# A diffusion block and a state-space block on one core: the turn of the attention probabilities moved to a third step of its unit

## The reference, cut to what matters

```python
for l in range(DEPTH):                    # DEPTH = 2
    with_ctx = l < DEPTH - 1              # 256 context tokens take part as queries in layer 0 only
    p  = jnp.split(n @ w_in[l], split_points, axis=-1)
    pc = jnp.split(nc @ w_in[l], split_points, axis=-1)
    oa, oa_c = diff_attention(...)          # "diff": two softmaxes per head, subtracted
    ob, ob_c = window_attention(...)        # "win": 2 key heads, a sink logit
    on, on_c = neighborhood_attention(...)  # "na": bias and mask
    od, od_c = qknorm_attention(...)        # "qk": normed q and k, 2 key heads
    y = (jnp.concatenate([oa, ob, on, od], axis=-1) * jax.nn.silu(p[12])) @ w_out[l]
    h = h + gate[:, None] * rms_norm(y, post_norm_g[l])
```

## Time and profile before

| | |
|---|---|
| median of 3 runs | 3108.85 us (3107.84 to 3115.51) |
| the profiled execution, its own time | 3112.07 us |
| its span in the profile | 3110.3 us |
| mean granted TensorE clock | 0.958 |
| PE busy | 2926.6 us, 94% of the span |
| DVE, ACT, POOL busy | 1937.8, 1164.8, 354.0 us |

### The profile page before, as it was taken

How to read it: one execution, slowest core, us unless ns; L and a number is a source line. 1 busy time by engine, 2 the same in 40 slices (tenths; PEclk the granted TensorE clock), 3 DMA queues, 4 the chain that set the end, 5 groups by cost and what they waited for, 6 DMA issues and landing times. The chain is left out here.

```text
span 3110.3 us, 40412 instructions
## 1 busy us (share of the span) xinstructions
PE 2926.6 (94%) x15557; PEld 2367.4 (76%) x15557; DVE 1937.8 (62%) x3393; ACT 1164.8 (37%) x1870; POOL 354.0 (11%) x317
## 2 busy tenths in 40 slices
PE   7989899999989997999999999989999999999998
PEld 2447677787767775868787777755789999999886
DVE  3238778676777767462445557875866666666444
ACT  3233332323323334242433443333344444444443
POOL 5760000000000000000000003532400000000000
PEclk9999999999999998999999998985899999999999
DMA  9846246353344564333333454420244555555554
GB/s 337 277 147 233 96 139 203 104 172 107 123 141 163 191 235 159 132 100 106 117 114 109 138 169 139 137 93 19 90 149 152 181 183 190 184 180 189 194 191 154
DMA packets 154592, 484.79 MB, mean 156 GB/s; under 512 B 17168, under 2 KB 18192, under 8 KB 153232
## 3 DMA queue, kind: packets, MB, share of 16 engines
q1 hardware_dynamic: 139968, 439.42, 42.2%
q10 hardware_dynamic: 14432, 42.79, 4.0%
HBM read 469.03 MB, written 13.11 MB: 155 GB/s over the span
## 5 line engine op out<-in xcount | busy, mean ns | idle before, releaser
L1484 DVE TENSOR_TENSOR split_weights<-common,split_weights 128x1024 fp32r<-128x1024 f32 x644 | 797.5, 1247 | 599.2 <-ACT split_weights L2211 551.5
L2211 ACT ACTIVATE split_weights<-common 128x1024 fp32r<-128x1024 f32 x644 | 671.4, 1052 | 812.6 <-PE bank L1160 752.1
L1158 PE MATMUL bank<-split_weights,features 128*128 128x512 f32 x1920 | 807.4, 421 | 48.9 <-DVE split_weights L1484 19.5
L1160 PE MATMUL bank<-split_weights,features 128*128 128x512 f32 x1920 | 760.7, 396 | 0.0
L1159 PE MATMUL bank<-split_weights,features 128*128 128x512 f32 x1920 | 760.0, 396 | 0.0
L1158 PEld LDWEIGHTS bank<-split_weights,features 128*128 128x128 f32 x1920 | 367.9, 192 | 163.7 <-issue 48.6
L1160 PEld LDWEIGHTS bank<-split_weights,features 128*128 128x128 f32 x1920 | 367.0, 191 | 80.7
L1159 PEld LDWEIGHTS bank<-split_weights,features 128*128 128x128 f32 x1920 | 368.1, 192 | 78.3 <-issue 11.3
L1607 DVE CUSTOM_DVE_ANT_0 common<-first_block_work,common 128x512 f32<-128x512 f32 x448 | 336.2, 751 | 92.3 <-DMA first_block_work<-w_mod_cols 75.1
L1158 PE MATMUL bank<-ffn_input_split,split_weights 128*128 128x256 f32 (+1 forms) x1376 | 389.8, 283 | 0.8 <-issue 0.8
L1160 PE MATMUL bank<-ffn_input_split,split_weights 128*128 128x256 f32 (+1 forms) x1376 | 389.0, 283 | 0.0
(11 more groups left out here) (295 smaller groups left out, 3396.3 us busy)
## 6 DMA issues: line engine op xcount, KB each, us to landing
common<-w_in SPq DMA_DIRECT2D x260, 512.0 KB, 3.4
common<-w_up SPq DMA_DIRECT2D x172, 512.0 KB, 4.3
first_block_work<-w_mod_cols SPq DMA_DIRECT2D x256, 256.0 KB, 3.8
common<-w_out SPq DMA_DIRECT2D x104, 512.0 KB, 3.3
common<-w_down SPq DMA_DIRECT2D x84, 512.0 KB, 3.4
old_stream<-w_mod SPq DMA_DIRECT2D x64, 512.0 KB, 4.7
trig<-common ACTq DMA_DIRECT2D x32, 272.0 KB, 4.4
second_block_work<-trig ACTq DMA_DIRECT2D x32, 272.0 KB, 2.7
```

The costliest lines, as they stand in the source:

```text
L1158: e.matmul(out_ap, xs[0], ws[0], start=first, stop=False)
L1160: return e.matmul(out_ap, xs[0], ws[1], start=False, stop=last)
L1484: e.tensor_tensor(lo, raw, hi.bitcast(F32), ALU.subtract).then_inc(*low_done.tick(("lo", m)))
L2211: e.activation(split_slots[:, 0, i, 0:words], raw_slots[:, m % RAW, 0:words], ACT.Copy).then_inc(*high_done.tick(("high", m)))
```

## The change

A unit of attention now comes in three steps: scores of unit i, then the values of unit i-2 (with `heads_out`), then the transposes of unit i-1. Pace, projections and all other work stay as they are. An attention has 54 steps in layer 0 and 30 in layer 1.

```diff
@@ -553,8 +553,6 @@
                     self.do("scores", n, l, g, kind, kvh, t, h, self.pb if biased else None)
             self.scale_heads()
             yield
-            if 0 <= i - 1 < len(units):
-                self.do("turn_probs", first + i - 1, units[i - 1][0], self.copies(), kind)
             if 0 <= i - 2 < len(units):
                 t, h = units[i - 2]
                 self.do("values", first + i - 2, l, g, kvh, t, h)
@@ -568,6 +566,9 @@
                     self.do("heads_out", first + i - 2, l, g, kind, t, r)
                     if kind == "diff":
                         self.unscaled.append(("heads_scaled", first + i - 2, l, g, t, r))
+            yield
+            if 0 <= i - 1 < len(units):
+                self.do("turn_probs", first + i - 1, units[i - 1][0], self.copies(), kind)
             yield
         self.scale_heads()
```

## The result

The change takes 3122.58 us in the median (12 runs, 3116.18 to 3128.71), the kernel before on the same chip 3110.03 us (12 runs, 3103.49 to 3115.95): ratio 1.0039, 95% interval 1.003 to 1.0049. It is slower by 12.5 us. The profiled execution of the change took 3128.71 us (span 3126.6, mean granted clock 0.954), 6 us above its median; that of before 3112.07 us, 2 us above. So between the two profiles lie 16.3 us of span, and I lean on a second profile of the change (span 3121.2) wherever a few us matter. Lines behind the edit are one higher in the change than before (1273 is now 1274). A "tail" is what is left of an attention when the products it hides between are through.

What follows compares the result with a forecast made beforehand. PE, busy 94% of the span, was taken to bound the kernel. Costs of 34.7 us, mostly tails, less a gain of 25 us gave +9.7 us: 3118.6 us in the median, range 3103 to 3136.

Steps and rivals of the forecast that it cites:

- Place 2's tail: End of layer 0's place 2 attention: 15.3 us of PE idle, first wait about 9 us, on ACT's copy.
- Rival A: Faster: tails flow, PE idles under 3 us in layer 0's place 2 tail; 3096 us, chance 0.11.
- What that tail saves later: After layer 0's place 2 tail: later PE waits on q's heads, 1.07 and 4.49 us, saved; 5.6 us.
- Place 3's tail: End of layer 0's place 3: about 17 us long, about 10 us idle; cost 9.0 us with the clock.
- Place 1: Layer 0's place 1: 3.8 us of its 4.9 us wait gained, tail costing 2.5 us.
- rival B: Waits stay because they come from DVE's backlog; gain 12 us for 25, time 3131 us; chance 0.15.
- Place 0: Layer 0's place 0: 4.7 us of waits gained, 1.9 of the 8.36 us scores' wait; tail costs 4.5 us.
- Layer 1: Layer 1's attention: waits of 4.8, 2.3 and 3.2 us gained in places 0 to 2; tails 5.3 and 2.2 us.
- The background "at nothing": Background's end moves from clock 1278 to about 1320, some 16 advances lost in layer 0; costed at nothing.
- rival C: Background dot products come later, where DVE feeds projections; 12 of 19 us show, 3131 us; chance 0.09.
- Rival D: Clock falls in every tail: 4 x 2.5 us more, 3129 us; chance 0.13.

Runs made afterwards that it cites:

- e3: The change with the steps left of layer 0's place 2 attention taken ahead of the first q tile's finish: 3103.37 us, 0.9984 of before.
- e11: The change with three more background advances, at clocks 701, 717 and 733 of layer 0, shifting every later row switch: 3106.6 us, 0.9993 of before.
- e4: Three steps only in layer 1's places 0 and 1, two steps everywhere else: 3100.19 us, 0.9973 of before.
- e8: e4 with the background held for the 24 clocks ahead of layer 0's places 0 and 1: 3083.32 us, 0.9922 of before.
- e2: The change with the background advanced at the clocks of the kernel before: 3123.40 us, 1.0047 of before.
- e9: The kernel before, two steps a unit, with the change's later background up to clock 816: 3103.09 us, 0.9976 of before.
- e10: The change with the edits of e3 and e2 together: 3120.11 us, 1.0039 of before.

## Why the prediction was right, and where it was wrong

The forecast was 3118.6 us and the likeliest case a small loss; measured are 3122.6 us and +0.40%. The sign and the size came out, but the size by luck: three stretches of the table were wrong by 7 to 13 us, one of them in the other direction, and they happened to cancel.

- **Place 2's tail: right.** Forecast 15.3 us idle, first wait about 9 us ending with the copy on ACT; measured 13.7 and 10.57, ending there. With 2.5 us of clock, 17.8 us against 17.1 and 15.1. e3 shows that the queue order makes most of it. Rival A falls.
- **What that tail saves later: mis-sized, 5.6 us for about 14.** I took two waits, on the heads of q. Before had four more at the start of the gate's projection, on the heads of k that pass the same DVE queue one projection later:

```profile
887.53 0.80 PE L1158 MATMUL bank<-split_weights,features 128*128 128x512 f32 x1 [8.45 <-ACT first_block_work L2348]
891.08 0.50 PE L1158 MATMUL bank<-split_weights,features 128*128 128x512 f32 x1 [0.62 <-ACT first_block_work L2348]
896.01 0.41 PE L1235 MATMUL bank<-common,first_block_work 128*128 128x128 f32 x2 [1.66 <-ACT old_stream L2359]
899.45 0.41 PE L1235 MATMUL bank<-common,first_block_work 128*128 128x128 f32 x2 [1.63 <-ACT old_stream L2359]
```

  With 1.07 and 4.49 that is 17.9 us of waits; after, the change has 3.5 us in their place, here:

```profile
894.42 0.50 PE L1159 MATMUL bank<-split_weights,features 128*128 128x512 f32 x1 [1.27 <-ACT first_block_work L2349]
897.97 0.50 PE L1159 MATMUL bank<-split_weights,features 128*128 128x512 f32 x1 [1.89 <-ACT first_block_work L2349]
906.68 0.44 PE L1236 MATMUL bank<-common,first_block_work 128*128 128x128 f32 x2 [0.36 <-DVE first_block_work L1703]
```

  PE that arrives later at a late DVE waits less by as much, and e3, which arrives earlier, has 11.0 us of later waits on these heads again (4.06, 6.29 and 0.62). So the heavy tail was nearly free in idle time.
- **Place 3's tail: over-sized.** Forecast about 10 us idle, 9.0 us with the clock and less the old end; the five waits of the tail sum to 5.3 us. From the last product to the last values it lasted 15 us for the 17 forecast, but 10 us of that were PE's own work, for 6.8. With the two points above, clocks 816 to 944 gave -8.8 where +3.4 was forecast.
- **Place 1: the 3.8 us weren't gained.** The wait was 4.33 us for 4.90. One profile settles little here: it was 3.5 us in the change's second profile and 1.84 us in e11's, whose instructions are the same up to there, and e4, which doesn't touch layer 0, had 6.54 us. So rival B holds for this wait in part; e8 shows the backlog. The tail cost 2.7 us as forecast (2.5). The stretch came out 7 us worse than its terms, of which 4 us are within what two profiles differ by; the rest is open.
- **Place 0: right.** The scores' wait fell by 1.95 us (forecast 1.9), the covered waits are gone, and the tail idled 2.1 us for 4.5.
- **Layer 1: right in the sums.** Place 0 gained 7.8 us for 7.6 with the clock, but split otherwise. At its end a wait of 1.62 us came where I had counted nothing, so the waits gave less than the 4.8 us and the clock more than the 2.8. Those 2.8 us don't follow from their own working either, which gives half of 3.4 us. Place 1 gained 2.4 for 2.3; place 2's wait was 6.08 for 5.3 (but the clock went with it), place 3 cost 1.7 for 2.2.
- **The background "at nothing": the step that failed, 8 to 10 us.** I priced when its dot products run (rival C: DVE where it feeds the projections), and set it at nothing because DVE is busy 62% of the whole span. By the planner the background is 13 advances behind at clock 816 and 9 at 944 (forecast 16 and 12). e2 and e9 refute the price of rival C: later is no loss, and in e9 a gain. Its sign didn't come either: PE's waits on lines 1484 and 1650 were 5.7 and 2.9 us before and are 5.5 and 3.6 us now (lines 1485 and 1651). What cost was where the advances fall: with three of them moved, which moves every later row switch, the same attention runs at 0.9993 (e11). That it is the switches and their loads is argued. The forecast landed because the gain it missed at clocks 816 to 944 (12 to 13 us) stood against this loss and place 1's, and that is luck.
- **Rival D**, the clock: it fell in the tails of places 1 and 2, in place 3's hardly; see the end.

So what does the third step do? Where it is covered it gains 8.5 us (e4). In the whole kernel it costs, and how much hangs on the background beside it: 14.7 us with the background of before (e2), 12.5 us in the change. Against e9, which has two steps and the change's background up to clock 816, the change is 20 us slower and e11, with three advances moved, 5 us. Where the advances fall is worth as much again: 16 us between the change and e11, 7.5 us between before and e9, 17 us between e3 and e10. e11's 0.9993 is therefore not the worth of the third step alone.

What is not settled: which of the five switches costs what (e11 moved all later ones), why the change loses 10 us against e11 at clocks 1136 to 1360, where its waits for the row loads were 6.08 and 4.88 us (e11: 3.09 and 2.11), and why e9, with 24.4 us of waits on line 2260, is still fast. That the row switch acts through ACT's blocked queue is argued from rows; that the place of the background's advances moves the time by more than the change did is shown.

## What to carry to other kernels

A step that moves work out of its cover is priced at the end of its stage by what stands ahead of it in each queue, and then by *all* waits that follow on the same chain, since PE arriving later waits less there. Where one planner's clock drives several generators, a longer one shifts the phase of the others: look for their rare steps (a load followed at once by its use), and test a verdict of a few tenths of a per cent by shifting the phase before believing it. Here the better lever was elsewhere: holding optional DVE work back for 24 clocks ahead of the attention, together with the third step where it is covered, took 24 us off.

## What the runs showed of the hardware

The clock after short waits goes either way. Windows of the change: place 1's tail, place 2's tail, place 3's tail, and layer 1's place 0, where the earlier trace rows had 0.76.

```profile
650.00:664.00 14.00, 11.98 (x52) 9.24 (x53) 5.92 (x14) 3.76 (x8) 0.00 (x0) 0.76 0.15 56
```

```profile
832.00:846.00 14.00, 10.44 (x33) 8.14 (x34) 9.18 (x22) 3.74 (x11) 1.70 (x2) 0.50 0.11 37
963.00:982.00 19.00, 12.73 (x80) 10.19 (x79) 16.36 (x46) 6.03 (x18) 0.00 (x0) 0.91 0.36 106
...
1366.00:1380.00 14.00, 14.00 (x72) 10.23 (x71) 10.30 (x19) 7.58 (x14) 0.00 (x0) 1.00 0.31 112
```

Waits of 1.71, 0.47 and 0.52 us in place 1's tail put PE at the lower level (the values at 654.12 took 1.23 us for 0.71), while 0.78, 2.09, 1.43, 0.47 and 0.52 us in place 3's left the values behind each of them at 0.71 us. There only matmuls between 967 and 970.5 us ran slower, such as the values at 967.79 us with 1.17 us. After place 2's tail the matmuls of a product came 0.43 us apart, at 1.2 GHz, up to 847.5 us. The Trainium skill's rule that activity releases the half clock ("TensorE: Matmul & The Clock Gate", Part 1) fits the 1.00 of the last row, where the two waits are gone. In the prediction I read it as making every tail pay; place 3's tail, with 0.91, hardly did.

The other surprise is the spread of one load's time. Each load of `c_rows` is 512 KB and issued by ACT. The ten of the change took 3.3 us from issue to landing in the median, and the one issued at 982.09 us, with the DMA engines at 351 GB/s, 12.3 us. In e11 the one issued at 967.27 us, at 135 GB/s, was used after 3.2 us. That the other loads delayed it is argued from these numbers; no run varied them alone.
